# First modulation by column quarters in a two-block transformer kernel: VectorE alone from the second quarter on, masks and root moved

## The chip, the cores and the metric

One core of a Trainium2 chip runs the whole program: two transformer blocks on one sequence of 256 tokens, model width 2048, all in float32. The metric is device time in microseconds (us) of one execution; lower is better.

## The reference, cut to what matters

```
mod = silu(c) @ w_ada + b_ada             # 2048 x 12288, six sections
shift1, scale1, gate1, shift2, scale2, gate2 = split(mod, 6)
h = rms_norm(x, norm1_w) * (1 + scale1) + shift1
aq, ak, av, gq, gf, gi, gg = split(h @ w_in)          # seven parts of 1024 columns
attn = rms_norm(dilated_attention(rope(norm(aq)), rope(norm(ak)), av))
hg   = rms_norm(hgrn2(gq, gf, gi)) * silu(gg)         # gated linear recurrence
x = x + gate1 * (concat(attn, hg) @ w_out)
x = x + gate2 * (relu(mod2(rms_norm(x)) @ w_ff1)**2 @ w_ff2)
# then a second block: stick-breaking attention and another MLP
```

Only the first lines matter here: the projection input h needs `shift1` and `scale1`, which are 4096 columns of a product of a 2048-vector with 33.5 MB of `w_ada`.

## The kernel before, in words

Every large matrix product runs on TensorE in single-pass fp32r with a split of both sides: A = A_hi + A_lo and w = w_hi + w_lo, three matmuls for each tile (L257 to L259). A **chunk** is 512 rows by 512 columns of weights (1 MB): SyncE loads it to `raw` (`load`, L448), ScalarE rounds it to `w_hi` (`split_hi`, L243), VectorE takes the rest to `w_lo` (`split_lo`, L247), and TensorE does 24 matmuls with it. There are four slots, so load, w_hi and w_lo of a chunk wait for users of the chunk four before. Chunks are counted through the kernel. Chunks 0 to 11 are the first attention group (`at0_chunk`): three column blocks (q, k, v; b = 0, 1, 2) by four row blocks k, each of which needs a quarter of A. 12 to 23 are the second attention group, 24 to 55 the two groups of the recurrence. A **slot** s is the step of each engine's loop at which TensorE works on chunk s; the attention of a group (`at_stage`) is spread over the slots of the group behind it, and its norms (`at_own`) over its own last ones (`at_steps`): ScalarE squares, VectorE sums heads, GpSimd takes the power -0.5 (`power`), ScalarE scales by it, VectorE rotates, TensorE turns.

**The start.** `w_ada` for shift1 and scale1 comes by pieces through the SyncE queue: a piece is 128 rows with 1024 columns of each of the two sections (h = 0, 1: the column halves; k = 0 to 15: the rows), 1 MB, in a ring of four slots `ada_raw`. VectorE multiplies a piece by its entries of silu(c) and adds it to `MS` (L1087, L1089). Pieces named in `ADA_BY_PE` (three in the first half, two in the second) are multiplied by TensorE with one-column matmuls instead (`piece_sums`, L1669). SyncE issues a piece when its slot is free, in order; some chunks' loads stand between (`LOADS_AFTER`), some w_lo stand between VectorE's products (`LOW_AFTER`). When a half is summed, TensorE sums it over partitions and turns it into columns (`step_sums`, L1679), VectorE adds the bias (`step_modulation`, L1070, L1074). Eight steps give A, two row blocks of 128 each: TensorE transposes normalised X (L306), ScalarE scales and shifts from PSUM (L344) and rounds to A_hi (L347), VectorE gives A_lo (L364). Chunks 0 to 5 use the first half of A, 6 to 11 the second, in the order of `AT0_ORDER`.

VectorE also does, ahead of the first piece, the attention's counts and masks (L949 to L970), and between pieces the five level masks of the recurrence (L1005), X's row squares and root (L1018) and the bounds and angles (L1029).

From slot 7 on, the other w_ada columns (gate1, shift2, scale2) come in 0.5 MB pieces through X's memory, two for each slot (`ada_pieces`); VectorE adds them (L1141, L1144: 128x1024).

## Time and profile before

| | |
|---|---|
| median of 3 runs | 2432.97 us (2432.86 to 2433.14) |
| the profiled execution | 2433.19 us |
| its span in the trace | 2431.4 us |
| mean granted TensorE clock | 0.988 |

The profile is one execution. Times in its rows are from the start of the span; "idle before" and an arrow name what ended an engine's wait. Where a row groups instructions, the second number is the time from the first one's start to the last one's end.

### The profile page before, as it was taken

Reading aid. Unit: us, or ns where it says so; the run is one execution under the profiler, and the core shown is the slowest. Engines: PE = TensorE matmul, PEld = TensorE weight load, DVE = VectorE, ACT = ScalarE, POOL = GpSimd, SP = SyncE. Lnnn points to the kernel's source line nnn. Section 1 sums busy time; section 2 is a strip of 40 time slices with the busy share of each in tenths; the row PEclk is TensorE's granted clock in tenths of the full one; section 3 lists DMA queues with packets and bytes.
Section 4 is the critical chain, followed back from the end, with each engine's and each line's share of the span. In section 5 each row is a group of like instructions: output and inputs, shape, how many; then the busy total and the mean of one; then the engine's idle time right before and its main releaser. Section 6 shows DMA issues by size and latency. Waiting matters only on the chain.

```text
span 2431.4 us, 27934 instructions
## 1 busy us (share of the span) xinstructions
PE 2359.0 (97%) x10954; PEld 1968.0 (81%) x10954; DVE 1594.6 (66%) x1284; ACT 1039.6 (43%) x890; POOL 51.4 (2%) x56
## 2 busy tenths in 40 slices
PE   4899999999999999999999999999999999999999
PEld 3777888887888888888887888878888888888887
DVE  7868989987666666655568456556555565565554
ACT  2245553435333333333334556664443433433432
POOL 1011000001000000000000000000000000000000
PEclk9789999999999999999999999999999999999999
DMA  9988987755676776655554545444555655555552
GB/s 355 362 300 311 361 311 268 252 199 169 231 241 231 234 242 224 224 190 181 183 190 171 177 160 168 156 138 158 183 191 183 191 184 192 189 188 190 190 189 104
DMA packets 235129, 520.30 MB, mean 214 GB/s; under 512 B 9705, under 2 KB 10162, under 8 KB 232370
## 3 DMA queue, kind: packets, MB, share of 16 engines
q1 hardware_dynamic: 234352, 519.15, 63.2%
q8 instruction: 49, 0.80, 0.1%
q10 hardware_dynamic: 706, 0.17, 0.0%
q14 instruction: 22, 0.18, 0.0%
HBM read 517.19 MB, written 2.10 MB: 214 GB/s over the span
## 4 chain that ended last, share of the span: by engine, by line
PE 90%; DVE 4%; DMA 2%; ACT 2%; issue 1%; DVEq 1%; POOL 1%; ACTq 0%; SPq 0%
PE PS L257 28%; PE PS L259 28%; PE PS L258 28%; DMA ada_raw<-in_w_ada_dram 2%; PE PS L1695 2%; PE PS L1734 1%; PE PS L1669 1%; DVE w_lo L247 1%; PE PS L306 1%; ACT w_hi L243 1%; POOL rstd L609 1%; PE PS L1679 1%; DVE ada_acc L1144 0%; DVEq L1511 0%; PE PS L1799 0%
## 5 line engine op out<-in xcount | busy, mean ns | idle before, releaser
L247 DVE TENSOR_TENSOR w_lo<-raw,w_hi 128x2048 fp32r<-128x2048 f32 x392 | 897.6, 2291 | 688.4 <-ACT w_hi L243 683.4
L243 ACT ACTIVATE w_hi<-raw 128x2048 fp32r<-128x2048 f32 x392 | 750.9, 1916 | 1149.1 <-PE PS L259 1137.7
L257 PE MATMUL PS<-w_hi,A_hi 128*128 128x512 f32 x2112 | 839.7, 398 | 10.0 <-DVE A_lo L361 3.5
L259 PE MATMUL PS<-w_hi,A_lo 128*128 128x512 f32 x2112 | 827.5, 392 | 0.0
L258 PE MATMUL PS<-w_lo,A_hi 128*128 128x512 f32 x2112 | 827.2, 392 | 0.0
L257 PEld LDWEIGHTS PS<-w_hi,A_hi 128*128 128x128 f32 x2112 | 400.6, 190 | 92.2 <-ACT qT L738 2.8
L259 PEld LDWEIGHTS PS<-w_hi,A_lo 128*128 128x128 f32 x2112 | 399.5, 189 | 84.9
L258 PEld LDWEIGHTS PS<-w_lo,A_hi 128*128 128x128 f32 x2112 | 400.4, 190 | 81.2 <-issue 1.0
L257 PE MATMUL PS<-w_hi,H_hi 128*128 128x512 f32 x1024 | 401.6, 392 | 2.0 <-issue 1.3
L259 PE MATMUL PS<-w_hi,H_lo 128*128 128x512 f32 x1024 | 398.9, 390 | 0.0
L258 PE MATMUL PS<-w_lo,H_hi 128*128 128x512 f32 x1024 | 398.5, 389 | 0.0
L257 PEld LDWEIGHTS PS<-w_hi,H_hi 128*128 128x128 f32 x1024 | 192.3, 188 | 41.9 <-issue 2.2
L259 PEld LDWEIGHTS PS<-w_hi,H_lo 128*128 128x128 f32 x1024 | 192.2, 188 | 40.3
L258 PEld LDWEIGHTS PS<-w_lo,H_hi 128*128 128x128 f32 x1024 | 192.4, 188 | 38.9
L1144 DVE SCALAR_TENSOR_TENSOR ada_acc<-X,sc,ada_acc 128x1024 f32<-128x1024 f32 x90 | 115.3, 1281 | 4.5
L609 POOL TENSOR_TENSOR rstd<-ssq,mhalf 128x8 f32<-128x8 f32 x20 | 44.7, 2234 | 1666.3 <-DVE ssq L419 1399.8
L1506 DVE TENSOR_TENSOR ACC<-ACC,PS 128x1024 f32<-128x1024 f32 x60 | 72.8, 1214 | 0.0
L1506 DVE TENSOR_TENSOR X<-X,PS 128x1024 f32<-128x1024 f32 x60 | 72.8, 1213 | 0.0
L1089 DVE SCALAR_TENSOR_TENSOR MS<-ada_raw,sc,MS 128x2048 f32<-128x2048 f32 x25 | 58.8, 2350 | 14.8 <-DMA ada_raw<-in_w_ada_dram 14.1
L1669 PE MATMUL PS<-sc,ada_raw 128*128 128x1 f32 x160 | 29.9, 321 | 29.4 <-DMA ada_raw<-in_w_ada_dram 29.4
L1669 PEld LDWEIGHTS PS<-sc,ada_raw 128*128 128x128 f32 x160 | 29.8, 290 | 30.0 <-DMA ada_raw<-in_w_ada_dram 15.7
L1477 DVE SCALAR_TENSOR_TENSOR ada_acc<-gate_w,sc,ada_acc 128x2048 f32<-128x2048 f32 x16 | 37.6, 2352 | 4.0 <-issue 4.0
(267 smaller groups left out, 1108.0 us busy)
## 6 DMA issues: line engine op xcount, KB each, us to landing
raw<-in_w_ff_dram SPq DMA_DIRECT2D x128, 1024.0 KB, 5.3
raw<-in_mlp_w_in_dram SPq DMA_DIRECT2D x64, 1024.0 KB, 5.4
raw<-in_mlp_w_out_dram SPq DMA_DIRECT2D x64, 1024.0 KB, 5.0
raw<-in_w_in_dram SPq DMA_DIRECT2D x56, 1024.0 KB, 8.1
X<-in_w_ada_dram SPq DMA_DIRECT2D x96, 512.0 KB, 5.7
raw<-in_sb_w_qkv_dram SPq DMA_DIRECT2D x48, 1024.0 KB, 5.1
ada_raw<-in_w_ada_dram SPq DMA_DIRECT2D x32, 1024.0 KB, 9.8
raw<-in_w_out_dram SPq DMA_DIRECT2D x16, 1024.0 KB, 6.6
```

The lines of the kernel that those rows point to most:

```text
L243: act.activation(w_hi[:, j, :, :], raw[:, j, :, :], ACT.Copy).then_inc(hi_rdy, 1)
L247: dve.tensor_tensor(w_lo[:, j, :, :], raw[:, j, :, :], w_hi[:, j, :, :].bitcast(F32), ALU.subtract).then_inc(lo_rdy, 1)
L257: pe.matmul(bank(pair + t), h, w_hi[:, j, k, :], start=first, stop=False)
L258: pe.matmul(bank(pair + t), h, w_lo[:, j, k, :], start=False, stop=False)
L259: mm = pe.matmul(bank(pair + t), l, w_hi[:, j, k, :], start=False, stop=last)
L609: pool.tensor_tensor(rstd[:, :], ssq[:, :], mhalf[:, :], ALU.pow).then_inc(rstd_rdy, 1)
L1089: ins = dve.scalar_tensor_tensor(out=MS[:, 1 - h, :], in0=sl, scalar=sc[:, k:k + 1], in1=MS[:, 1 - h, :], op0=ALU.mult, op1=ALU.add)
L1144: ins = dve.scalar_tensor_tensor(out=acc, in0=ada_ring[:, q % CH, :], scalar=sc[:, k:k + 1], in1=acc, op0=ALU.mult, op1=ALU.add)
L1477: dve.scalar_tensor_tensor(out=acc, in0=gate_w[:, half, :], scalar=c, in1=acc, op0=ALU.mult, op1=ALU.add).then_inc(gate_w_used, 1)
L1506: dve.tensor_tensor(ac, ac, PS[:, b:b + 2, :], ALU.add).then_inc(acc_read, 1)
L1669: mm = pe.matmul(bank(6, at, at + 1), ada_raw[:, k % CH, P * c:P * c + P], sc[:, k:k + 1], start=True, stop=True)
L1695: mm = pe.transpose(bank(first_bank + i, P * q, P * q + P), src[:, t, HD * h:HD * (h + 1)], ident[:, :])
```

## The change

- The first modulation goes by four column quarters of 512. A piece has 512 columns of each section, 0.5 MB; the ring has eight slots in the same memory. VectorE multiplies all but three pieces of the first quarter, which are TensorE's.
- For each quarter TensorE transposes the first of its two steps, sums the quarter (`quarter_sums`), in quarters 2 and 3 runs one chunk (2 and 5: the third that needs the quarter before), then transposes the second step once the modulation is there, and runs chunks 0 and 1; 3 and 4; 6, 7 and 8; none. Chunks 9 to 11 come behind the fourth quarter. `AT0_ORDER` is row block by row block. The chunk of column block 0 waits for A_lo in two parts.
- X's squares go to ScalarE; the root's arithmetic stands behind product (0,8). The level masks are drawn by GpSimd behind the first power. Counts and masks go to VectorE's slots 10 and 11. Bounds and angles stand at (2,5).
- Group 0's norm steps lie one to two slots later, both its turned tiles go through banks 6 and 7, its attention one slot later (`STAGE_LAG`); chunk 12 waits for the first scaling (`n_mul`).
- The 0.5 MB pieces of the other columns start at slot 10 instead of 7; slots 13, 21, 36, 37, 49 and 50 take three.

The core of the diff:

```diff
-AT0_ORDER = [(b, k) for h in range(2) for b in range(3) for k in (2 * h, 2 * h + 1)]
-HEAD = CH * 3 // 2
-ADA_BY_PE = (3, 7, 11), (7, 11)
-PRE_COLS = 0, 96
-SUM_AT = (0, 0), (6, 80), (6, 160), (7, 0)
-
-
-def ada_share(h, k, mine):
-
-    return sum((b in ADA_BY_PE[a]) == mine for a in range(2) for b in range(KT) if (a, b) <= (h, k))
-
-
-LOADS_AFTER = {(0, 9): 0, (0, 11): 1, (0, 13): 2, (1, 0): 3, (1, 2): 4, (1, 4): 5, (1, 6): 6, (1, 9): 7}
-LOW_AFTER = {(0, 12): 0, (0, 14): 1, (1, 2): 2, (1, 4): 3, (1, 6): 4, (1, 9): 5, (1, 10): 6, (1, 13): 7}
-
-
-HG1_SLOT = CH * (OUT0 - 4)
-LEVEL_SLOTS = (range(HG1_SLOT, HG1_SLOT + 7),) + 2 * (range(CH * OUT0 - 1, CH * OUT0 + 2),) + (range(CH * OUT0 + 3, CH * OUT0 + 4),)
+QUARTERS = D // NC_
+RING = 2 * CH
+AT0_ORDER = [(b, k) for k in range(QUARTERS) for b in range(3)]
+HEAD = 3 * (QUARTERS - 1)
+ADA_BY_PE = (3, 7, 11), (), (), ()
+STAGE_LAG = 1
+def ada_share(q, k, mine):
+    return sum((b in ADA_BY_PE[a]) == mine for a in range(QUARTERS) for b in range(KT) if (a, b) <= (q, k))
+LOADS_AFTER = {(0, 9): 0, (1, 0): 1, (1, 6): 2, (1, 10): 3, (2, 0): 4, (2, 5): 5, (2, 10): 6, (3, 0): 7, (3, 5): 8, (3, 10): 9}
+LOW_AFTER = {(0, 12): 0, (1, 4): 1, (1, 9): 2, (1, 14): 3, (2, 4): 4, (2, 9): 5, (2, 14): 6, (3, 4): 7, (3, 9): 8, (3, 14): 9}
+ADA_FROM = HEAD + 1
+ADA_NONE = range(CH * OUT0 - 1, CH * OUT0 + 2)
+ADA_ONE = tuple(range(CH * (OUT0 - 4), CH * (OUT0 - 4) + 7)) + (CH * OUT0 + 3,)
+ADA_THREE = 13, 21, 36, 37, 49, 50
...
+    def per(x):
+        return 0 if x < ADA_FROM or x in ADA_NONE else 1 if x in ADA_ONE else 3 if x in ADA_THREE else 2
+    first, last = sum(per(x) for x in range(slot)), 2 * ADA_SLOTS
+    return range(min(first, last), min(first + per(slot), last))
...
+QUARTER_BANKS = 6, 7
...
+        ada_slots = ada_raw[:, :, :].rearrange("p j (h n) -> p (j h) n", n=2 * NC_)
+        ada_sum_of = [setup[:, D + 2 * NC_ * i:D + 2 * NC_ * (i + 1)] for i in range(2)]
...
             b, k = AT0_ORDER[n]
-            if b == 0:
-                pe.wait_ge(a_lo, 2 * (k + 1))
-            chunk(pe, n // CH, n % CH, pairs[b], lambda i, t: A_hi[:, CH * k + i, P * t:P * t + P],
-                  lambda i, t: A_lo[:, CH * k + i, P * t:P * t + P], k == 0, k == CH - 1)
+            if b:
+                chunk(pe, n // CH, n % CH, pairs[b], lambda i, t: A_hi[:, CH * k + i, P * t:P * t + P],
+                      lambda i, t: A_lo[:, CH * k + i, P * t:P * t + P], k == 0, k == CH - 1)
+                return
+            j = n % CH
+            pe.wait_ge(lo_rdy, n + 1)
+            for i in range(CH):
+                if i % 2 == 0:
+                    pe.wait_ge(a_lo, 2 * k + i // 2 + 1)
+                for t in range(T):
+                    h, l = (x[:, CH * k + i, P * t:P * t + P] for x in (A_hi, A_lo))
+                    first, last = k == 0 and i == 0, k == CH - 1 and i == CH - 1
+                    pe.matmul(bank(pairs[b] + t), h, w_hi[:, j, i, :], start=first, stop=False)
+                    pe.matmul(bank(pairs[b] + t), h, w_lo[:, j, i, :], start=False, stop=False)
+                    mm = pe.matmul(bank(pairs[b] + t), l, w_hi[:, j, i, :], start=False, stop=last)
+            mm.then_inc(chunk_done, 1)
...
-                    sp.wait_ge(y_rdy, 4)
+                    sp.wait_ge(sum_rdy, 1)
...
+            for piece in range(QUARTERS * KT):
+                q, k = divmod(piece, KT)
+                if piece >= RING:
+                    q0, k0 = divmod(piece - RING, KT)
+                    if k0 in ADA_BY_PE[q0]:
+                        sp.wait_ge(ada_pe, ada_share(q0, k0, True))
+                    else:
+                        sp.wait_ge(ada_used, ada_share(q0, k0, False))
+                sp.dma_start(ada_slots[:, piece % RING, :].rearrange("p (s n) -> p s n", s=2),
+                             ada[:, k, 0:2, NC_ * q:NC_ * (q + 1)]).then_inc(ada_in[piece % RING], 16)
+                if (q, k) == (0, CH - 1):
+                    sp.dma_start(X[:, :, :], a["x"].rearrange("a (t p) d -> p (a t) d", p=P)).then_inc(x_in, 16)
+                if (q, k) in LOADS_AFTER:
+                    load_at0(LOADS_AFTER[q, k])
...
+            power(0)
+            for i, w in enumerate(LEVELS):
+                drawn = setup[:, 1024 + P * (i % 2):1024 + P * (i % 2 + 1)]
+                upper = drawn.rearrange("p (b two w) -> p b two w", two=2, w=w)[:, :, 1, :]
...
+                pool.tensor_copy(lv_mask[:, i, :], drawn).then_inc(level_drawn, 1)
+            for i in range(1, MIX_JOBS + 2):
...
+            act.wait_ge(x_in, 16)
+            act.wait_ge(ssq_set, 1)
+            for t in range(T):
+                act.activation(Y0[:, t, :], X[:, t, :], ACT.Square, accum_out=ssq[:, t:t + 1]).then_inc(row_sq, 1)
             act.wait_ge(rstd_rdy, POWER_OF[0])
             for c in range(4):
                 normalise(act, X, X, c)
-            for n in (0, 1):
-                split_hi(act, 0, n)
-            turn_act(act, 0, g1, mod[:, SHIFT1, :], turned, steps=ALL[:4], banks=FIRST)
-            for n in range(2, CH * 2):
-                split_hi(act, n // CH, n % CH)
-            turn_act(act, 0, g1, mod[:, SHIFT1, :], turned, steps=ALL[4:], first=4, banks=SECOND_STEPS,
-                     between={1: lambda: split_hi(act, 2, 0)})
-            split_hi(act, 2, 1)
+            split_hi(act, 0, 0)
+            for q in range(QUARTERS):
+                turn_act(act, 0, g1, mod[:, SHIFT1, :], turned, steps=(2 * q, 2 * q + 1), first=2 * q, banks=QUARTER_BANKS)
+                for n in range(3 * q + 1, 3 * q + 4):
+                    split_hi(act, n // CH, n % CH)
...
+            def counts():
+                dve.wait_ge(level_drawn, 5 * len(LEVELS))
...
+            def masks():
...
+                dve.wait_ge(row_sq, T)
...
+            def quarter_modulation(q):
+                n = len(ADA_BY_PE[q]) + 1
+                r0, kts = RA["norm1"][0] + 4 * q, slice(4 * q, 4 * q + 4)
+                sums = ada_part[:, q, 0:8]
+                dve.wait_ge(ada_pe, ada_share(q, KT - 1, True))
+                dve.wait_ge(ada_sum, q + 1)
+                dve.tensor_reduce(sums, bank(QUARTER_BANKS[1], 0, 8 * n).rearrange("p (c m) -> p c m", m=n), AX_X, ALU.add)
+                d()
+                dve.tensor_tensor(mod[:, SHIFT1:GATE1, kts], sums.rearrange("p (s k) -> p s k", s=2),
+                                  colA[:, 0:2 * KT].rearrange("p (s k) -> p s k", s=2)[:, :, kts],
                                   ALU.add).then_inc(mod_rdy, 1)
                 d()
                 dve.scalar_tensor_tensor(out=g1[:, kts], in0=mod[:, SCALE1, kts], scalar=1.0, in1=colA[:, r0:r0 + 4],
                                          op0=ALU.add, op1=ALU.mult).then_inc(g_rdy, 1)
+            def turn_first(step):
+                turn_dve(dve, 0, g1, mod[:, SHIFT1, :], turned, steps=(step,), first=step,
+                         banks=QUARTER_BANKS[step % 2:step % 2 + 1], tmp_at=step % 2)
...
+            for q in range(QUARTERS):
                 for k in range(KT):
+                    if k in ADA_BY_PE[q]:
                         continue
+                    piece = KT * q + k
+                    sl, acc = ada_slots[:, piece % RING, :], ada_sum_of[q % 2]
+                    dve.wait_ge(ada_in[piece % RING], 16 * (piece // RING + 1))
                     if k == 0:
+                        ins = dve.tensor_scalar(acc, sl, sc[:, k:k + 1], None, ALU.mult)
                     else:
+                        ins = dve.scalar_tensor_tensor(out=acc, in0=sl, scalar=sc[:, k:k + 1], in1=acc, op0=ALU.mult, op1=ALU.add)
                     ins.then_inc(ada_used, 1)
+                    if (q, k) == (0, 8):
                         first_root()
+                    if q and k == 0:
+                        quarter_modulation(q - 1)
+                    if q and k in (1, 2):
+                        turn_first(2 * (q - 1) + k - 1)
+                    if (q, k) == (2, 5):
                         dve.wait_ge(rstd_rdy, 1)
                         bounds_and_angles()
+                    if (q, k) in LOW_AFTER:
+                        n = LOW_AFTER[q, k]
                         split_lo(dve, n // CH, n % CH)
+                    dve.wait_ge(ada_used, ada_share(q, k, False))
...
+            for step in (KT // 2 - 2, KT // 2 - 1):
+                turn_first(step)
+            for n in range(len(LOW_AFTER), CH * 3):
+                split_lo(dve, n // CH, n % CH)
...
-                            at_stage(pi, s, False, None)
+                            at_stage(pi, s - STAGE_LAG * (i == 1), False, None)
+                    if i == 0 and s == HEAD + 1:
+                        counts()
+                    if i == 0 and s == HEAD + 2:
+                        masks()
+                    if i == 1:
+                        at_own(0, PROJ0, CH * 3 + s, True)
...
+            def quarter_sums(q):
+                n = len(ADA_BY_PE[q]) + 1
+                pe.wait_ge(ada_used, ada_share(q, KT - 1, False))
+                for c in range(8):
+                    at = n * c + n - 1
+                    mm = pe.matmul(bank(QUARTER_BANKS[1], at, at + 1), ada_sum_of[q % 2][:, P * c:P * c + P], ones[:, 0:1],
+                                   start=True, stop=True)
                 mm.then_inc(ada_sum, 1)
...
+            for q in range(QUARTERS):
+                for k in ADA_BY_PE[q]:
+                    piece_sums(q, k)
+                pe.wait_ge(y_rdy, q + 1)
+                turn(0, X, steps=(2 * q,), first=2 * q, banks=QUARTER_BANKS[:1])
+                quarter_sums(q)
+                if q in (1, 2):
+                    at0_chunk(pe, 3 * q - 1)
+                pe.wait_ge(mod_rdy, q + 1)
+                turn(0, X, steps=(2 * q + 1,), first=2 * q + 1, banks=QUARTER_BANKS[1:])
+                for n in ((0, 1), (3, 4), (6, 7, 8), ())[q]:
+                    at0_chunk(pe, n)
...
+                        if i == 1 and s == 0:
+                            pe.wait_ge(n_mul, 1)
+                            used[p] += 1
+                        elif s % CH == 0:
...
-        return {"square": (8, 10), "norm": (9, 11), "turn": (10, 12), "copy": (11, 12)}
+        return {"square": (10, 11), "norm": (11, 12), "turn": (12, 13), "copy": (13, 13)}
...
+    return (6, 6) if isinstance(n, int) and n == 0 else (0, 2)
```

## Rows read from the trace of the kernel before

**Rows 1.** The page: busy times, and the costliest groups of instructions.
```profile
PE 2359.0 (97%) x10954; PEld 1968.0 (81%) x10954; DVE 1594.6 (66%) x1284; ACT 1039.6 (43%) x890; POOL 51.4 (2%) x56
...
L247 DVE TENSOR_TENSOR w_lo<-raw,w_hi 128x2048 fp32r<-128x2048 f32 x392 | 897.6, 2291 | 688.4 <-ACT w_hi L243 683.4
L243 ACT ACTIVATE w_hi<-raw 128x2048 fp32r<-128x2048 f32 x392 | 750.9, 1916 | 1149.1 <-PE PS L259 1137.7
...
L1144 DVE SCALAR_TENSOR_TENSOR ada_acc<-X,sc,ada_acc 128x1024 f32<-128x1024 f32 x90 | 115.3, 1281 | 4.5
```
**Rows 2.** Busy time by windows: length, PE, PEld, DVE, ACT, POOL, PEclk, DMA share, GB/s.
```profile
85.00:110.00 25.00, 25.00 (x114) 21.10 (x113) 24.80 (x12) 6.56 (x4) 0.00 (x0) 0.86 1.01 392
110.00:120.00 10.00, 10.00 (x55) 9.03 (x55) 9.36 (x5) 1.11 (x1) 0.00 (x0) 0.83 0.45 181
...
125.00:131.00 6.00, 4.55 (x32) 3.88 (x30) 2.11 (x3) 1.04 (x3) 0.00 (x0) 0.94 1.05 409
```
**Rows 3.** VectorE in order of time: start, us, instruction, idle before.
```profile
4.00 0.36 DVE L952 TENSOR_SCALAR MS<-MS 128x384 int32<-128x384 int32 x1 [3.05 <-POOL MS L604]
...
10.65 0.28 DVE L974 COPY colA<-PS 128x128 f32<-128x128 f32 x1
...
19.89 0.28 DVE L1007 TENSOR_TENSOR MS<-MS 128x128 int32<-128x128 int32 x1
...
24.45 2.29 DVE L1022 CUSTOM_DVE_ANT_0 raw<-X 128x2048 f32<-128x2048 f32 x1
...
29.15 7.13 DVE L1089 SCALAR_TENSOR_TENSOR MS<-ada_raw,sc,MS 128x2048 f32<-128x2048 f32 x3
...
43.62 0.16 DVE L1032 TENSOR_TENSOR turned<-turned 128x8 f32<-128x8 f32 x1
...
45.73 0.06 DVE L1049 MEMSET w_cols<- 32x2 f32 x1
...
72.91 0.17 DVE L1070 TENSOR_TENSOR mod<-PS,ada_part 128x8 f32<-128x8 f32 x1 [2.34 <-PE PS L1679]
...
76.84 1.29 DVE L364 TENSOR_TENSOR A_lo<-turned,A_hi 128x512 fp32r<-128x512 f32 x2
...
124.43 2.35 DVE L1089 SCALAR_TENSOR_TENSOR MS<-ada_raw,sc,MS 128x2048 f32<-128x2048 f32 x1 [3.96 <-DMA ada_raw<-in_w_ada_dram]
...
163.56 2.66 DVE L1144 SCALAR_TENSOR_TENSOR ada_acc<-X,sc,ada_acc 128x1024 f32<-128x1024 f32 x2
```
**Rows 4.** TensorE in order of time.
```profile
69.30 6.99 PE L1679 MATMUL PS<-ones,MS 128*128 128x1 f32 x32 [10.28 <-DVE MS L1089]
...
136.70 0.78 PE L257 MATMUL PS<-w_hi,A_hi 128*128 128x512 f32 x1
...
174.70 0.79 PE L257 MATMUL PS<-w_hi,A_hi 128*128 128x512 f32 x1 [2.41 <-ACT qT L738]
...
222.52 0.90 PE L1786 MATMUL PS<-ident,E 128*128 128x128 f32 x3 [2.85 <-ACT E L780]
```
**Rows 5.** The chain that ended last, in order of time: start, us, what.
```profile
177.63 0.43 PE PS L257
...
179.28 0.23 PE PS L257
```
**Rows 6.** ScalarE in order of time.
```profile
33.05 5.01 ACT L317 ACTIVATE X<-X,rstd 128x512 f32<-128x512 f32 x8 [18.53 <-POOL rstd L609]
...
73.44 1.02 ACT L344 ACTIVATE turned<-PS,mod,g 128x256 f32<-128x256 f32 x2 [20.13 <-DVE g L1074]
74.53 0.63 ACT L347 ACTIVATE A_hi<-turned 128x512 fp32r<-128x512 f32 x1
...
157.77 2.17 ACT L713 ACTIVATE QN<-PS,rstd 128x128 f32<-128x128 f32 x8 [0.69 <-POOL rstd L609]
```
**Rows 7.** GpSimd in order of time.
```profile
29.29 3.72 POOL L609 TENSOR_TENSOR rstd<-ssq,mhalf 128x8 f32<-128x8 f32 x1 [25.32 <-DVE ssq L1025]
```
**Rows 8.** A window around slots 49 and 50, columns as in rows 2.
```profile
425.00:450.00 25.00, 25.00 (x139) 21.53 (x138) 23.21 (x22) 11.24 (x12) 1.64 (x1) 1.00 0.77 267
```

More of the change, by code:

```diff
@@ L350, in turn_act, with turn_dve @@
                     between[pos]()
-        def turn_dve(dve, n, g, s=None, tmp=None, steps=ALL, first=0, banks=WIDE, between=None):
+        def turn_dve(dve, n, g, s=None, tmp=None, steps=ALL, first=0, banks=WIDE, between=None, tmp_at=0):
             dve.drain()
@@ L1075, in step_modulation @@
                                          op0=ALU.add, op1=ALU.mult).then_inc(g_rdy, 1)
-            def turn_first(steps, first, **more):
-                turn_dve(dve, 0, g1, mod[:, SHIFT1, :], turned, steps=steps, first=first, **more)
-            for h in range(2):
+            def turn_first(step):
+                turn_dve(dve, 0, g1, mod[:, SHIFT1, :], turned, steps=(step,), first=step,
+                         banks=QUARTER_BANKS[step % 2:step % 2 + 1], tmp_at=step % 2)
+            for q in range(QUARTERS):
```

201 lines of the change are left out of this document (57 added, 144 removed).

## The prediction

> **What bounds the kernel now.** Read the page first: TensorE is busy for 2359.0 us, 97% of the span [rows 1]. So only where TensorE idles, runs at its low clock or does work that could go away can time be won, and nearly all of that lies before the last modulation of projection input A. The edit is wholly in that start and in the first groups behind it.
>
> Next the windows [rows 2]. From 85 to 110 us VectorE is busy 24.8 of 25 us while DMA moves 392 GB/s: both are near their limits. From 110 to 120 DMA falls to 181 GB/s. The in-order SyncE queue explains it: piece (1,15) may go out only when TensorE's product of piece (1,11) has freed the slot, and that product stands behind the fifth chunk. The last product therefore starts at 124.43 and ends at 126.78, after 3.96 us of waiting for its load [rows 3]. Then come sums, A's second half, and six chunks from 136.70 to 172.29, where the next stall (2.41 us) begins [rows 4].
>
> Small prices. A matmul follows the last one after 0.43 us at 1.2 GHz and after 0.23 us at 2.4 GHz [rows 5]. A chunk of 24 is 5.46 us at the high clock. Six are 32.8; the 35.6 us from 136.70 to 172.29 leave 2.8, the turning of QN and some 9 slow matmuls at 0.2 more each: about 2 us, to be paid whenever TensorE has idled for over 2 us. After its 2.41 and 2.85 us of idleness the next matmul was slow again [rows 4].
>
> **What the change saves.** When the last product ends, three chunks are left instead of six: 3 x 5.46 = 16.4 us off the path. Between last product and first chunk lay 136.70 - 126.78 = 9.9 us (two sets of sums, four steps). Now: sums of one quarter 3.5 us (16 records; 32 took 6.99 [rows 4]), reduce, modulation and scale 0.65 (from the add at 72.91 to ScalarE's start at 73.44 it was 0.53, and a reduce of 0.2 more is my estimate), shift and copy on ScalarE 1.02 + 0.63 and gaps 0.2, A_lo half of 1.29 [rows 3, 6]: 6.7 us, since chunk 9 starts with its first step. That saves 3.2 us more. The change wins if the last product ends less than 19.6 us after 126.78.
>
> **When the last product ends.** It is a chain on VectorE.
>
> Its load: 61 products of 128x1024. That form took 1281 ns [rows 1], and two in a row 2.66 [rows 3], so 1.28 to 1.38 from start to start; I take 1.33, as this same loop left gaps of 0.04 at 2048 columns (three in 7.13 [rows 3]). The bounds give -3 and +3 us over 57 of them. Before, 27 products of 2.39 were 64 us; now 57 of 1.33 and four first ones of about 0.8 are 79. Two halves cost 0.27 us more than the one they replace, and TensorE's five pieces shrink to three halves. Ten w_lo instead of eight stand before the end, at 2.29 us [rows 1], 2.2 from start to start. Removed in front: masks 4.00 to 10.65, level masks 19.89 to 24.45, squares to 29.1, some 15.8 us [rows 3]. But these lay where the loads set the pace, so they buy little.
>
> First quarter. X now has 2.1 MB less before it: at about 0.41 MB/us that is 5.1 us before 24.45, so 19.4. ScalarE squares twice, bounded by one w_hi pass each (1.92 [rows 1]; with an accumulator 2.1): 23.5. The root stands behind product (0,8), whose load lies five pieces (6.3 us) behind X: 27.3. Pow 3.72 [rows 7], four normalisations 5.01 [rows 6], w_hi(0) 1.92: 38.0. w_lo(0) stands in VectorE's queue behind (0,12), whose load lies four pieces and one of w_in (7.6 us) behind (0,8)'s and which is done at 34.7; VectorE waits 3.3 us, and products 13 to 15 wait behind it. w_lo 2.3 and three products 4.0: the quarter ends at 44.3. Were w_hi(0) there in time, it would be 41.
>
> Each later quarter, from the end e of the last. The first product (0.8) hides in the sums, at e+3.65; modulation to e+4.2; product 1 to e+5.5; A_hi at e+6.05, A_lo to e+6.7; product 2 to e+8.05; second A_lo to e+8.7. Thirteen products 17.3 and three w_lo 6.6: 32.6 us.
>
> In quarters 3 and 4 there is something else: chunks 2 and 5 stand on TensorE between the sums and the second step's turning. VectorE waits for that step's A_hi right after product 2. TensorE has idled some 12 us (its chunks of the quarter before are done 17 us into a quarter of 32), so the chunk costs 7.3 us: e+3.55+7.3, transposes 0.5, ScalarE 1.8, gives A_hi at e+13.1 where VectorE wants it at e+8.05. That is 5.1 us twice, with all products and splits behind it. If the chunk ran at the high clock throughout, 3.2 twice.
>
> Quarter 3 has the bounds and angles too, 2.2 us (43.62 to 45.79 [rows 3]). So: 44.3 + 32.6 + (32.6+5.1+2.2) + (32.6+5.1) = 154.5 us. Does DMA hold it up? A quarter needs 8.4 MB of pieces and three chunks of w_in, 11.5 MB: 28 us at 0.41. Its packets shrink from 4 to 2 KB, but the window 125 to 131, when only 2 KB rows of w_in were moved, shows 409 GB/s [rows 2]. No: VectorE's 32.6 is longer. SyncE's added waits (loads 4 to 9 of w_in wait for w_lo four chunks back, in front of later pieces) pass at once by the order of splits: each w_lo wanted lies over eight pieces earlier, the ring's depth.
>
> **Up to chunk 12.** First chunk at 161.2, three chunks with 2 us of low clock: 179.6. Chunk 12 now waits for the first ScalarE scaling of QN (banks are turned elsewhere). VectorE does A_lo to e+8.7, w_lo of 10, 11, 12 (the first waits 0.9 for ScalarE) to e+16.3, then the counts (seven of the fourteen mask instructions, about 3.7 of the 6.65 us) with the head sum of 1.5 behind them: e+21.5. Pow 3.7 and norm 2.17 [rows 6, 7]: 181.9. So 2.3 us stall, as 2.41 before [rows 4]; chunk 12 starts at 182.0 instead of 174.70: 7.3 us late. Counts and masks are taken from 4 us, where nothing hung on them, and lie here, where VectorE has no slack.
>
> **Behind it.** Slots 12 to 23 of the first group's attention. VectorE starts them later than before against TensorE: 3 us of masks, and two slots of three pieces (2.7 us). Before, one wait of TensorE for a softmax row of 2.85 us stood there [rows 4]. I expect one more of the kind, with slow matmuls 4.5, and 0.7 at KN's bank: 5.2. Bounds: 0, if slack takes it all, and 10 for two more. The other four extra pieces (5.3 us) lie in slots 36, 37, 49, 50; VectorE was busy 23.2 of 25 us around the last two while TensorE never idled [rows 8]. I take them as hidden by what VectorE runs ahead: 0, and 5.3 if that cover is gone. Level masks on GpSimd run while VectorE waits: 0.
>
> One thing on that. Pow on GpSimd ran from 29.29 to 33.0 beside three VectorE products that kept 2.35 each [rows 3, 7]. The Trainium skill (SBUF — State Buffer, "Who interferes with whom") says that a VectorE instruction with two SBUF inputs and a GpSimd instruction that reads SBUF exclude each other for the whole instruction. By that rule the first quarter would lose up to the 3.7 us of pow, and the time would be 2449. This trace doesn't agree, so the sum stays with 0.
>
> **Sum.** 7.3 + 5.2 = 12.5 us later. The profiled execution took 2433.19 us (span 2431.4 and 1.8 around it), 0.22 above the median of 2432.97; 2432.97 + 12.5 = 2445.5.
>
> **Rivals.**
> (a) VectorE keeps pace with the loads: faster. By DMA alone the 46 MB up to piece (3,15) end at about 122, the last product at 124. Then 16.4 + 3.2 + 3 would be won, less 2 to 5 behind: 2413. For it: DMA and VectorE were both nearly full before [rows 2], and of the two only VectorE's share can be read wrongly by its waits. Against: 79 us of products, 23 of w_lo and the waits. It decides when the last product ends before about 140.
> (b) Same: w_hi(0) is early (-3), third chunks run fast (-4), and no further stall in the attention (-5): about 2434 to 2437.
> (c) Slower by more: VectorE stays the bound in slots 12 to 50, two further softmax stalls and the four pieces exposed: 12.5 + 5 + 5 = 22, 2455. For it: VectorE's 23.2 of 25 us [rows 8]. Against: TensorE's clock there was 1.00 throughout.
> (d) The change doesn't do what it says: chunks 6 to 8 don't fit before the last sums. Chunk 8 needs its w_lo after (3,9), done 10 us before the end; it fits. If one were left, +5.5: 2451.
>
> **Chances.** Forecast (2440 to 2450) 0.5; (b) 0.17; (c) and (d) 0.2; (a) 0.13. The range leaves out most of (a) and the far end of (c): 2431 to 2456. A difference under 0.2% (4.9 us) can't be told from none. Faster 0.12; same 0.14, most of (b); slower 0.74.
>
> **What the profile will show.** VectorE's first-quarter products end near 44, the others near 77, 117, 154. Rows of A_lo waiting 5 us on A_hi twice. TensorE: a chunk right behind sums at 80 and 120; idle about 12 us before both; chunk 9 near 161, chunk 12 near 182 with a stall of 2 us. Behind the second group all starts 12 to 13 us later than before, by a constant shift. I am wrong if the last product ends before 145, if a product of 1024 columns takes far from 1.33, or if the shift still grows after 270 us.

## The result and the profile after

The changed kernel takes 2448.26 us (median of 3 runs, 2448.22 to 2449.42) against 2432.97: ratio 1.0066, 95% interval [1.0049, 1.0083], slower by 15.3 us. The forecast was 12.5 us.

The page of the changed kernel, the lines that answer to [rows 1]. TensorE is 15 us less busy in a span 15 us longer, so its idle time grew by 30 us. Half of that is busy time that it no longer has: 112 matmuls fewer, those of its pieces (five of 32 matmuls before, 29.9 us; three of 16 now, 10.7 us). The products of 1024 columns take 1284 ns, and 17.6 us is all that VectorE waited in front of them.
```profile
PE 2344.1 (96%) x10842; PEld 1947.1 (80%) x10842; DVE 1601.2 (65%) x1302; ACT 1042.5 (43%) x894; POOL 63.0 (3%) x79
...
L252 DVE TENSOR_TENSOR w_lo<-raw,w_hi 128x2048 fp32r<-128x2048 f32 x392 | 897.5, 2291 | 682.3 <-ACT w_hi L248 677.1
...
L1103 DVE SCALAR_TENSOR_TENSOR MS<-ada_raw,sc,MS 128x1024 f32<-128x1024 f32 x57 | 73.2, 1284 | 17.6 <-DMA ada_raw<-in_w_ada_dram 14.7
```
Its windows, two of those of [rows 2] and the one of [rows 8]. From 85 to 110 us VectorE was busy 24.8 of 25 us before and now 19.4, and DMA moves 234 GB/s where it moved 392: both stand and wait for something else.
```profile
85.00:110.00 25.00, 15.40 (x70) 12.01 (x69) 19.43 (x32) 7.06 (x6) 0.00 (x0) 0.90 0.71 234
110.00:120.00 10.00, 3.10 (x15) 3.10 (x15) 7.53 (x6) 0.00 (x0) 0.00 (x0) 0.50 1.05 405
...
425.00:450.00 25.00, 25.00 (x137) 21.61 (x137) 23.15 (x20) 11.07 (x10) 0.00 (x0) 1.00 0.87 307
```
VectorE in order of time shows what it waits for. At 38.31 the first w_lo waits for ScalarE, with the quarter's last three products behind it. At 90.43 and 130.65 the second A_lo of quarters 3 and 4 waits for A_hi. The last products of quarters 2 to 4 start at 75.96, 115.57 and 153.96.
```profile
38.31 2.37 DVE L252 TENSOR_TENSOR w_lo<-raw,w_hi 128x2048 fp32r<-128x2048 f32 x1 [1.97 <-ACT w_hi L248]
...
75.96 1.28 DVE L1103 SCALAR_TENSOR_TENSOR MS<-ada_raw,sc,MS 128x1024 f32<-128x1024 f32 x1
...
90.43 0.69 DVE L381 TENSOR_TENSOR A_lo<-turned,A_hi 128x512 fp32r<-128x512 f32 x1 [4.80 <-ACT A_hi L364]
...
115.57 1.28 DVE L1103 SCALAR_TENSOR_TENSOR MS<-ada_raw,sc,MS 128x1024 f32<-128x1024 f32 x1
...
130.65 0.69 DVE L381 TENSOR_TENSOR A_lo<-turned,A_hi 128x512 fp32r<-128x512 f32 x1 [5.41 <-ACT A_hi L364]
...
153.96 1.28 DVE L1103 SCALAR_TENSOR_TENSOR MS<-ada_raw,sc,MS 128x1024 f32<-128x1024 f32 x1
...
174.47 1.22 DVE L1272 TENSOR_REDUCE ssq<-QN 128x8 f32<-128x1024 f32 x1
...
175.85 2.28 DVE L252 TENSOR_TENSOR w_lo<-raw,w_hi 128x2048 fp32r<-128x2048 f32 x1
```
TensorE in order of time, to be read with [rows 4]: two long idle times before sums, chunk 9 at 161.64, chunk 12 at 181.89 (174.70 before), then three more waits in the first group's attention.
```profile
77.29 3.57 PE L1696 MATMUL PS<-ones,MS 128*128 128x1 f32 x16 [11.48 <-DVE MS L1103]
...
116.91 3.58 PE L1696 MATMUL PS<-ones,MS 128*128 128x1 f32 x16 [14.58 <-DVE MS L1103]
...
161.64 0.77 PE L299 MATMUL PS<-w_hi,A_hi 128*128 128x512 f32 x1 [1.77 <-DVE A_lo L381]
...
181.89 0.50 PE L262 MATMUL PS<-w_hi,A_hi 128*128 128x512 f32 x1 [1.50 <-ACT QN L746]
...
195.84 1.06 PE L1713 MATMUL PS<-ident,KN 128*128 128x128 f32 x8 [1.81 <-ACT qT L771]
211.11 0.90 PE L1806 MATMUL PS<-ident,E 128*128 128x128 f32 x3 [2.62 <-ACT E L813]
240.96 0.55 PE L1806 MATMUL PS<-ident,E 128*128 128x128 f32 x3 [3.02 <-ACT E L813]
...
268.06 1.03 PE L1713 MATMUL PS<-ident,KN 128*128 128x128 f32 x8
287.13 0.55 PE L1806 MATMUL PS<-ident,E 128*128 128x128 f32 x3 [1.02 <-ACT E L813]
...
445.86 1.04 PE L1713 MATMUL PS<-ident,QN 128*128 128x128 f32 x8
```
The last two of these turnings in the kernel before are those of KN at 255 us and of a later QN. The shift is 7.2 us at chunk 12, 13.0 at KN, 15.4 at 446 us, and 15.1 over the span.
```profile
255.02 1.03 PE L1695 MATMUL PS<-ident,KN 128*128 128x128 f32 x8
...
430.47 1.04 PE L1695 MATMUL PS<-ident,QN 128*128 128x128 f32 x8
```

### The profile page after: what moved, and what is told of

Same layout as the page of the kernel before. It is cut to its first block, busy times and chain, and to the rows that moved or that the text cites. A ratio compares the mean times of both kernels' runs of the same rounds, so it can differ in the third digit from the quotient of the medians.

```text
span 2446.5 us, 27826 instructions
## 1 busy us (share of the span) xinstructions
PE 2344.1 (96%) x10842; PEld 1947.1 (80%) x10842; DVE 1601.2 (65%) x1302; ACT 1042.5 (43%) x894; POOL 63.0 (3%) x79
## 4 chain that ended last, share of the span: by engine, by line
PE 84%; DVE 8%; issue 3%; ACT 2%; DVEq 1%; DMA 1%; POOL 0%; ACTq 0%; SPq 0%
PE PS L262 26%; PE PS L264 26%; PE PS L263 26%; DVE MS L1103 2%; DVE w_lo L252 2%; PE PS L1713 2%; DVE ada_acc L1152 1%; PE PS L1752 1%; DMA ada_raw<-in_w_ada_dram 1%; ACT w_hi L248 1%; PE PS L1696 1%; PE PS L323 0%; POOL rstd L624 0%; DVEq L1527 0%; PE PS L1819 0%
## 5 line engine op out<-in xcount | busy, mean ns | idle before, releaser
L262 PE MATMUL PS<-w_hi,A_hi 128*128 128x512 f32 x2080 | 825.7, 397 | 14.5 <-DVE w_lo L252 7.2
L264 PE MATMUL PS<-w_hi,A_lo 128*128 128x512 f32 x2080 | 814.1, 391 | 0.0
L263 PE MATMUL PS<-w_lo,A_hi 128*128 128x512 f32 x2080 | 813.9, 391 | 0.0
L262 PEld LDWEIGHTS PS<-w_hi,A_hi 128*128 128x128 f32 x2080 | 393.4, 189 | 97.0 <-DVE w_lo L252 8.4
L264 PEld LDWEIGHTS PS<-w_hi,A_lo 128*128 128x128 f32 x2080 | 392.8, 189 | 83.5
L263 PEld LDWEIGHTS PS<-w_lo,A_hi 128*128 128x128 f32 x2080 | 393.3, 189 | 79.8 <-issue 1.0
L1103 DVE SCALAR_TENSOR_TENSOR MS<-ada_raw,sc,MS 128x1024 f32<-128x1024 f32 x57 | 73.2, 1284 | 17.6 <-DMA ada_raw<-in_w_ada_dram 14.7
L1696 PE MATMUL PS<-ones,MS 128*128 128x1 f32 x64 | 13.6, 342 | 34.5 <-DVE MS L1103 34.5
L361 ACT ACTIVATE turned<-PS,mod,g 128x256 f32<-128x256 f32 x16 | 8.1, 557 | 89.4 <-DVE g L1086 78.3
L1696 PEld LDWEIGHTS PS<-ones,MS 128*128 128x128 f32 x64 | 13.2, 315 | 35.7 <-DVE MS L1103 35.7
```

What stands on the lines that cost most here:

```text
L262: pe.matmul(bank(pair + t), h, w_hi[:, j, k, :], start=first, stop=False)
L263: pe.matmul(bank(pair + t), h, w_lo[:, j, k, :], start=False, stop=False)
L264: mm = pe.matmul(bank(pair + t), l, w_hi[:, j, k, :], start=False, stop=last)
L1103: ins = dve.scalar_tensor_tensor(out=acc, in0=sl, scalar=sc[:, k:k + 1], in1=acc, op0=ALU.mult, op1=ALU.add)
L1696: mm = pe.matmul(bank(QUARTER_BANKS[1], at, at + 1), ada_sum_of[q % 2][:, P * c:P * c + P], ones[:, 0:1], start=True, stop=True)
```

## The experiments

My theory was the prediction's: in the start VectorE is one chain; the third chunk of quarters 1 and 2 holds it up twice, masks and counts come at a bad place, and the 16 us of chunks taken off the path don't pay for that. The rivals are that DMA with its smaller packets sets the pace, or that TensorE does. Each ratio below is to the kernel before, run beside that version. With 3 or 4 runs of a version its interval reaches some 4 us to each side. So where two such versions lie 2 us apart, their times don't show the difference, and only the rows can tell where it comes from.

**The third chunk before the sums.**
```
-                if q in (1, 2):
-                    at0_chunk(pe, 3 * q - 1)
-                for n in ((0, 1), (3, 4), (6, 7, 8), ())[q]:
+                for n in ((0, 1, 2), (3, 4, 5), (6, 7, 8), ())[q]:
```


> Undoes one part of the change: chunks 2 and 5 of the first projection run before the next quarter's sums instead of between them and the second step's turning. My theory (VectorE is a chain in the start, and the third chunk holds back its A_lo twice): the waits of 4.80 us at 90.43 and 5.41 us at 130.65 vanish, VectorE's last product ends near 144 instead of 155.2, chunk 12 starts near 171 to 172, and the whole shift of about 10 us stays through the second group: about 2438 us. Rival 1 (VectorE's lateness is only in appearance; w_lo and the pieces of the loads set the pace, so something else ends last): the two waits vanish, but VectorE waits for loads in their place and the last product still ends after 150: 2444 or more. Rival 2 (the third chunk hid in time in which TensorE would idle anyway, so moving it before the sums makes TensorE late for the sums): the sums begin later than VectorE's last product of a quarter and nothing is won: about 2448.

Measured: 2438.28 us (2435.41 to 2441.06, 10 runs), ratio 1.0023 [1.0013, 1.0032]. The waits of 4.80 and 5.41 us are gone; the last sums start at 143.61, for which 144 was expected, and chunk 9 at 150.67. The theory holds and both rivals fall; the interval lies wholly below that of the changed kernel. But the lead isn't kept: at KN this kernel is only 0.5 us behind the kernel before, at 436.48 it is 6.0 us behind, after another softmax wait. Its TensorE rows:
```profile
143.61 3.58 PE L1696 MATMUL PS<-ones,MS 128*128 128x1 f32 x16 [3.66 <-DVE MS L1103]
150.67 0.77 PE L299 MATMUL PS<-w_hi,A_hi 128*128 128x512 f32 x1 [1.78 <-DVE A_lo L381]
...
255.50 1.04 PE L1713 MATMUL PS<-ident,KN 128*128 128x128 f32 x8
...
276.18 0.90 PE L1806 MATMUL PS<-ident,E 128*128 128x128 f32 x3 [2.63 <-ACT E L813]
...
436.48 1.04 PE L1713 MATMUL PS<-ident,QN 128*128 128x128 f32 x8
```

**Counts and masks in front.**
```
+            dve.wait_ge(pool_const, N_CONST)
+            counts()
+            masks()
...
-                    if i == 0 and s == HEAD + 1:
-                        counts()
-                    if i == 0 and s == HEAD + 2:
-                        masks()
```


> Undoes one part of the change: counts and masks are made by VectorE at about 4 us, as in the kernel before, instead of in the first group's slots. My theory: the quarters end as in the changed kernel (44.5, 77.2, 116.9, 155.2, each within 0.5), the head sum comes 3.6 us earlier, so the stall of 1.50 us before chunk 12 goes, and with the masks out of slot 14 the wait at the turning of KN of the second group is reached 3 to 5 us earlier: 2443.5 to 2445.5. Rival 1 (this work also hides beside something here): the stall goes, but the softmax waits of 2.62 and 3.02 us grow by as much: 2447 to 2449. Rival 2 (the front isn't free: VectorE's first products or the squares wait for it): the first quarter ends later by up to 6 us, and the time is 2448 to 2452.

Measured: 2445.92 us (1.0055 [1.0038, 1.0072]), 2.3 us less than the changed kernel, which the intervals don't separate. In the rows the stall before chunk 12 is gone and KN of the second group turns at 264.59 (3.5 us earlier), but the second softmax wait grew from 3.02 to 4.45 us. The places are the theory's; its range (2443.5 to 2445.5) is missed by 0.4 us, and some of rival 1 is in it.

**TensorE multiplies two pieces of each quarter.**
```
-ADA_BY_PE = (3, 7, 11), (), (), ()
+ADA_BY_PE = (3, 7, 11), (7, 11), (7, 11), (7, 11)
```


> Undoes one part of the change: TensorE multiplies pieces 7 and 11 of quarters 2, 3 and 4 too, so VectorE has 6 products of about 1.3 us fewer. Theory A (VectorE's own work sets the start's length from product to product): the last product ends 7 to 8 us earlier and the time is about 2440 to 2441. Theory B (the same chain, but a slot that TensorE reads comes free only when TensorE comes to it, and pieces 7 and 11 are read before the quarter's first step, so the fewer products only bring VectorE sooner to waits for loads or for A_hi, which still hang on the sums and the third chunk): quarter ends 2 to 5 us earlier, time 2443 to 2446. Rival (TensorE's reading of the pieces stands in front of its turning, waits for loads and delays the second step by more than it saves): no gain or a loss, 2448 to 2455.

Measured: 2446.48 us (1.0058 [1.0041, 1.0075]). This is theory B, a little outside its ranges (2 to 5 us, 2443 to 2446): sums of quarters 2, 3 and 4 start 2.8, 5.4 and 4.8 us earlier (74.52, 111.50, 150.47), and VectorE now waits 3.85 us for a load before its last product. Six products less gave 1.8 us in the end, which the intervals don't separate from none.

**All three.**
The edits of the three experiments above together.

> Undoes three parts at once: the third chunk before the next sums, masks and counts in front, TensorE multiplying two pieces of each quarter. What remains is the split into four quarters with the squares on ScalarE, the level masks on GpSimd and the later turning. My theory, the shifts being separate and added as far as the loads let them: the last product ends near 140, chunk 12 starts near 164 to 166, the shift against the changed kernel is 16 to 18 us: 2430 to 2433, level with the kernel before or a little under. Rival 1 (with VectorE relieved, DMA sets the end of the start): the last product still ends after 145 with VectorE waiting for loads for 5 us and more in quarters 3 and 4: 2436 to 2442. Rival 2 (four quarters win outright once VectorE is relieved, 16 us of chunks being off the path): under 2425.

Measured: 2443.57 us (1.0046 [1.0029, 1.0063]). My sum of 2430 to 2433 failed: this version is 5 us slower than the one with the third chunk alone. Rival 1 named the place (loads late in quarters 3 and 4), but its range of 2436 to 2442 is missed too. VectorE waits for loads in quarters 2 to 4:
```profile
77.41 1.28 DVE L1105 SCALAR_TENSOR_TENSOR MS<-ada_raw,sc,MS 128x1024 f32<-128x1024 f32 x1 [3.88 <-DMA ada_raw<-in_w_ada_dram]
...
115.27 1.28 DVE L1105 SCALAR_TENSOR_TENSOR MS<-ada_raw,sc,MS 128x1024 f32<-128x1024 f32 x1 [5.50 <-DMA ada_raw<-in_w_ada_dram]
...
150.39 1.28 DVE L1105 SCALAR_TENSOR_TENSOR MS<-ada_raw,sc,MS 128x1024 f32<-128x1024 f32 x1 [2.25 <-DMA ada_raw<-in_w_ada_dram]
```
By its name this is a shortage of DMA. The waits of SyncE's queue from 20 to 170 us say otherwise: 40.8 us in which the next load waited for TensorE's reading of an old piece.
```profile
SPq L484 <- PE PS L1684: 40.8, 5, 13.5
```

**Third chunk and masks, VectorE alone.** The edits of the first two experiments together.

> Undoes two parts of the change (third chunk before the next sums, counts and masks in front at 4 us), and keeps the third: VectorE alone multiplies from the second quarter on. Together with the version that undid all three (2443.6 us, last product late because VectorE waited for loads 3.88, 5.50 and 2.25 us) it isolates TensorE's pieces. Theory A (a slot that TensorE is to read stands behind a chunk in TensorE's queue, and so holds back the loads behind it; with VectorE alone the slots come free in time): the loads are there, last product near 144 as with the third chunk alone, and the two gains add: 2435 to 2437 us. Rival B (masks in front cost more here, because they make the squares and the first loads late once nothing else is): 2438 to 2440. Rival C (what held the version with all three was DMA itself and not the slots): VectorE waits for loads here as well, last product after 148, 2441 or more.

Measured: 2433.74 us (2430.48 to 2435.89, 11 runs), 1.0002 [0.9993, 1.0011], better than the sum of the two and than the 2435 to 2437 expected. The last sums start at 143.44 (151.73 with TensorE's pieces), no product after 40 us waits a microsecond for its load, and the same row of SyncE's queue is:
```profile
SPq L484 <- PE PS L1684: 3.1, 2, 1.6
```
So theory A holds. TensorE's pieces gave 1.8 us in the kernel that had the third chunk late, and cost 10 us in this one, since a chunk then stands in TensorE's queue before the reading that frees the slot. VectorE alone from the second quarter on is the part of the change that is worth having here.

This version also prices the masks a second time: against the one with the third chunk alone they are the only difference, 2438.28 to 2433.74 us, and these intervals lie apart. The third softmax wait fell from 2.63 us (at 276.18) to 1.03 (at 272.16), the shift at KN by 2.4 us and at the later QN by 5.6.

**Two slots of three pieces later.**
```
-ADA_THREE = 13, 21, 36, 37, 49, 50
+ADA_THREE = 30, 33, 36, 37, 49, 50
```


> As the one before (third chunk before the sums, masks in front), and the two slots of three pieces that lie at 13 and 21, between the first softmax rows, are moved to 30 and 33. The number of pieces is the same. Theory A (from chunk 12 to 25 VectorE has no slack: a w_lo of 2.2 and two products of 2.67 per chunk of 5.46, and each row of softmax that it makes late stops TensorE for some 2.6 us and brings back the low clock): at least one of the three softmax waits seen in the version with the third chunk alone (200.16, 230.01, 276.18) goes or all shrink, 2 to 4 us less than the version before: 2432 to 2434. Rival B (these waits are the chain transposition, softmax on ScalarE and back, whatever VectorE does): the same waits, the same time within 1 us. Rival C (the pieces hurt as much at 30 and 33): the wait at 276 grows, time the same or up to 2 us more.

Measured: 2433.88 us (1.0003 [0.9994, 1.0012]), no difference from the version before. The two softmax waits were 1.22 and 4.63 instead of 2.61 and 3.14, a third of 1.03 vanished, and at KN the profiled execution was 3.1 us ahead (249.96 to 253.08), of which 1.2 were there at chunk 9 already. Then this stood at 371 us:
```profile
371.43 2.05 PE L1750 MATMUL PS<-bT,kT 128*128 128x128 f32 x16 [2.65 <-DVE kT L1209]
```
The time lies in theory A's range (2432 to 2434), but only because the version before was faster than that range took for granted: the 2 to 4 us between them aren't there, and the lead at KN is given back at the wait at 371 us.

**The same move in the changed kernel.** (The same one-line edit.)

> The changed kernel with one move: the slots of three pieces at 13 and 21 lie at 30 and 33. Tests my term of 5.2 us for waits in the first group's attention (measured 2.62 at 211.11, 3.02 at 240.96, 1.02 at 287.13). Theory A (two products of 1.33 us in slots without slack cause part of these waits): second group's KN turned 2 to 3 us earlier than 268.06. Rival B (VectorE's whole amount of work up to slot 48 is what counts, so the lead is given back): KN at 268 earlier by 2 to 3 but a wait of 2 to 3 us appears at 370 to 390 and the time is within 1 us of 2448.3. If theory A alone: 2445 to 2446.5. If neither: KN at 268.

Measured: 2449.94 us (1.0076 [1.0061, 1.0092]); KN at 267.70, only 0.4 earlier, waits of 1.21 and 4.63 where there were 2.62 and 3.02, and 2.65 at 389.20. It is not faster; rival B's return of the lead is seen, on a lead that was hardly there. The slots of three pieces decide which of the two softmax waits is the long one, and not their sum (5.84 us here, 5.64 in the changed kernel).

**w_lo of chunk 0 behind product (0,15).**
```
-LOW_AFTER = {(0, 12): 0, (1, 4): 1, (1, 9): 2, (1, 14): 3,
+LOW_AFTER = {(0, 15): 0, (1, 4): 1, (1, 9): 2, (1, 14): 3,
```


> The changed kernel with one move: w_lo of chunk 0 behind product (0,15) instead of (0,12). Tests my term for the first quarter: VectorE stood 1.97 us at w_lo(0) for ScalarE's w_hi(0), with three products and the quarter's sums behind it. Theory A (that wait and the split itself lie on the path of the first quarter): sums of quarter 1 start near 40.5 to 41.5 instead of 44.58, later quarters 3 to 4 us earlier throughout, about 2444.5 to 2446. Rival B (the loads of pieces 13 to 15 set that end): VectorE waits for loads instead, the sums start at 43 or later, within 1.5 us of 2448.3. Rival C (the gain is swallowed before the second quarter ends, since the loads of quarter 2 aren't there yet): quarter 1 ends early, quarter 2 ends at 76 or later.

Measured: 2446.32 us (1.0050 [1.0035, 1.0066]). Sums of quarter 1 start at 40.69 instead of 44.58, which is theory A at that place (its range of times, 2444.5 to 2446, is missed by 0.3 us). Of the 3.9 us, 3.1 are left at the last sums but one and 2.7 at the last, because the waits behind the third chunk grow (5.54 and 5.86), and 1.9 in the time, which the intervals don't separate from none.

**The kernel before, piece (1,11) read one chunk earlier.**
```
-                if n in (2, 4):
-                    piece_sums(1, ADA_BY_PE[1][n // 2 - 1])
+                if n in (2, 3):
+                    piece_sums(1, ADA_BY_PE[1][n - 2])
```


> The kernel before with one move: TensorE reads piece (1,11) behind its fourth chunk instead of its fifth. Tests the reading of the load that came late there (VectorE's last product waited 3.96 us for piece (1,15), which may go out only when piece (1,11) has been read). Theory A (the slot behind TensorE's chunk held the load back): the slot is free 5.5 us earlier, the wait of 3.96 us goes, the last product starts near 120.5 instead of 124.43, and as TensorE's sixth chunk then ends last (near 124.6), the sums start some 2 us earlier: 2430 to 2431 against 2432.4. Rival B (DMA was the limit and the slot of no matter): product (1,15) starts at 123 or later, time unchanged within 0.5 us. Rival C (piece (1,11) isn't there yet at 109 and TensorE waits for it): the sixth chunk ends later, 2433 to 2436.

Measured: 2431.65 us (11 runs), 0.9991 [0.9982, 1.0001], which can't be told from none. The mechanism shows: the last product has no wait any more and starts 2.56 us earlier (124.43 in [rows 3]), though all rows of this execution lie 1.1 us later from 70 us on. The wait of 3.96 us was the slot's, not DMA's. The sums that follow gained little (they start at 127.76 against 127.05, in an execution that lies 1.1 us later), because TensorE's sixth chunk ends just before them in both.
```profile
121.87 2.35 DVE L1089 SCALAR_TENSOR_TENSOR MS<-ada_raw,sc,MS 128x2048 f32<-128x2048 f32 x1
...
130.08 0.17 DVE L1070 TENSOR_TENSOR mod<-PS,ada_part 128x8 f32<-128x8 f32 x1 [5.86 <-PE PS L1679]
```

**What helped, together.** With the two slots moved:

> All that has helped so far: third chunk before the next sums, masks in front, the two slots of three pieces at 30 and 33, and w_lo of chunk 0 behind product (0,15). In the changed kernel the last move alone brought sums of quarter 1 from 44.58 to 40.69 us and 2 us in the end. Theory A (VectorE's stream sets the pace from the start to slot 48, so that what it gains in the first quarter stays): everything from the second quarter to 450 us lies 2.5 to 4 us earlier than in the version without the move (QN turned at 429.45 there), time 2430 to 2432, under the kernel before by 1 to 3 us. Rival B (loads of the second quarter or a row of softmax eat it): second quarter's sums at 77, or another wait near 371 us that grows: 2433 to 2435.

and with them in their place:

> Third chunk before the sums, masks in front, w_lo of chunk 0 behind (0,15), and the slots of three pieces where the changed kernel has them (13, 21). Against the version just before it tells what moving the two slots is worth, against the version without the move of w_lo (2433.7 us) what that move is worth. Theory A: 2 to 3 us under the 2433.7, 2431 to 2432. Rival B (the move gives nothing once the third chunk lies earlier): 2433.5 to 2434.5. If the slots at 30 and 33 only delay the same deficit of VectorE (a wait of 2.65 us appeared at 371 us there), both versions come out within 0.5 us of each other.

Measured: 2431.80 us, 0.9993 [0.9984, 1.0002], and 2430.51 us (2427.63 to 2431.21, 11 runs), 0.9989 [0.9980, 0.9998]. The second (third chunk before the sums, masks in front, w_lo(0) late) is the fastest, 2.3 us under the kernel before beside it, and 17.8 under the changed one. It isn't clear of the version with the slots moved (1.3 us), nor of the kernel before with piece (1,11) read earlier (2431.65 us, a change of two lines). The move of w_lo is worth 3.2 us there, by intervals that just overlap. Its rows: 
```profile
40.91 3.57 PE L1694 MATMUL PS<-ones,MS 128*128 128x1 f32 x16 [2.14 <-DVE MS L1105]
...
145.66 0.77 PE L299 MATMUL PS<-w_hi,A_hi 128*128 128x512 f32 x1 [1.77 <-DVE A_lo L381]
...
249.35 1.04 PE L1711 MATMUL PS<-ident,KN 128*128 128x128 f32 x8
...
427.15 1.04 PE L1711 MATMUL PS<-ident,QN 128*128 128x128 f32 x8
```
It starts chunk 12 at 164.70, 10.0 us ahead of the kernel before (174.70), reaches KN 5.7 us ahead, is 3.3 ahead at 427 us and 2.3 in the time. So the start in four quarters wins 10 us, and the slots behind it give three quarters of that back.

**VectorE waits for GpSimd's root.**
```
                 if s == steps["square"][0]:
                     head_norm(n, 0, QN, 0, 1.0 / SCALE ** 2, rotate, not rotate, meanwhile)
+                    if isinstance(n, int) and n == 0:
+                        dve.wait_ge(rstd_rdy, 2)
```


> The changed kernel; VectorE, after the first head sum of QN, waits for GpSimd's root before it goes on with w_lo of chunk 12. Tests whether GpSimd is kept waiting by VectorE. The root before head scaling of QN took 3.61 us (176.03) beside w_lo (175.85, 2.28 us), and the root at 354.78, beside which VectorE did nothing, 1.64. Theory A (GpSimd's root stands until VectorE's instruction with two operands is through, and VectorE loses nothing by it): the root takes 1.64, ends 2 us earlier, and chunk 12 starts up to 1.5 us earlier, without its stall of 1.50 us; VectorE is 1.8 us later behind it, which softmax waits may take back: 2446 to 2449. Theory B (the root takes 3.6 us in this place whatever VectorE does, its input or code being cold): 3.6 us again, VectorE 3.7 us later, 2448 to 2452.

Measured: 2450.28 us (1.0071 [1.0054, 1.0087]). The root took 1.64 us, and chunk 12 starts at 181.12 with no stall of a microsecond or more: theory A, in the mechanism. Its time lies above theory A's 2446 to 2449: KN's turning then waited 4.66 us instead of 1.81, VectorE being 2 us later with everything behind, and the version isn't faster than the changed one. The root in this kernel (first line), and in the changed one:
```profile
176.81 1.64 POOL L624 TENSOR_TENSOR rstd<-ssq,mhalf 128x8 f32<-128x8 f32 x1 [130.36 <-DVE ssq L1275]
```
```profile
176.03 3.61 POOL L624 TENSOR_TENSOR rstd<-ssq,mhalf 128x8 f32<-128x8 f32 x1 [130.25 <-DVE ssq L1275]
...
354.78 1.64 POOL L624 TENSOR_TENSOR rstd<-ssq,mhalf 128x8 f32<-128x8 f32 x1 [104.68 <-DVE ssq L436]
```

## Why the prediction was right, step by step

- **The chain on VectorE.** Forecast ends of the last products 44.3, 76.9, 117 and 154.5; measured 44.5, 77.2, 116.9 and 155.2. The start to start time of 1.33 us was 1.32 (five in 6.56). In the first quarter two errors cancelled: X's root was computed at 28.50 instead of 27.3, but its power took 2.69 us (at 28.74) and not the 3.72 of [rows 7], so that w_hi(0) was there at 38.3 where 38.0 was forecast. That product (0,12) came at 35.05 instead of 33.3 cost nothing: it only made the wait for w_hi(0) 1.97 us instead of 3.3. "Were w_hi(0) there in time, it would be 41" was shown by the move of w_lo (40.69), though there w_lo itself left the path too.
- **The third chunk.** Forecast 5.1 us twice, measured 4.80 and 5.41; taking it away gave 11.7 us at the last sums (155.29 to 143.61) and 10.0 in the time. It is the largest of the parts of the loss that were undone one by one. The chunk itself took 7.3 us and 7.9 (7.3 was taken), the first eight and eleven of its matmuls at a granted clock of 0.50.
- **DMA.** "No: VectorE's 32.6 is longer" holds: without TensorE's pieces and without the third chunk a quarter took 32.3 us (111.35 to 143.61 between its sums) and from the second quarter on no product waited as much as 0.7 us for a load.
- **Up to chunk 12.** Forecast 7.3 us late with a stall of 2.3; measured 7.2 and 1.50. The masks are behind the stall: with them in front it is gone. In the time they are worth 2.3 us alone, inside the intervals, and 4.5 us with the third chunk early, outside them. Chunk 12 came with no low clock behind that stall (matmuls 0.23 us apart from 182.24 on), which the sum hadn't counted on.
- **Behind it.** Forecast 5.2, measured 13.0 - 7.2 = 5.8: the turning of KN 1.81 (0.7 was taken), softmax 2.62 and 3.02 against one of 2.85. These waits are 4.6 of the 5.8 us; no wait of 0.6 us or more holds the rest. The number was near, and two of its reasons weren't right: the slots of three pieces moved away changed KN by 0.4 us, and the extra slow matmuls (4.5 - 2.85 = 1.65 of the 5.2 us) didn't come: 13 matmuls of 512 columns took 0.6 us or more in this stretch, and 13 in the kernel before.
- **Slots 24 to 62** is the term that was mis-sized: 0 taken, 5.3 as its bound; measured 15.4 - 13.0 = 2.4, of which 1.86 stand in a softmax wait of 1.02 at 287.13 and a wait for VectorE of 0.84 at 387.83; the rest is in no wait of that size. With it the sum would have been 14.9. The prediction names this as a sign of being wrong ("if the shift still grows after 270 us"), and it did grow: in the reading of these slots the prediction was wrong, and it was right in the number because the term is small. Every version with four quarters gives way in the same stretch (against the kernel before, 1.7 to 5.9 us between the turnings at 255 and 430 us). VectorE is busy 21 to 24 of 25 us in the windows from 250 to 450 us, in the changed kernel and in the fastest version, and so it is in the kernel before, where no such wait stands; moving its pieces to and fro gives nothing. That VectorE comes into this stretch late and can't catch up there is argued from this and not shown; nearest to a test comes the return of the masks, which takes work away from it ahead of the stretch and cut the growth from 5.5 us to 2.4 with the third chunk early, but left it (2.4 and 2.6 us) where that chunk came late.
- **The rule weighed.** The Trainium skill (SBUF — State Buffer, "Who interferes with whom") was set aside because VectorE's products kept their length. They did here too (1284 ns). But the sign was on the other engine: it is the row of 3.72 us in [rows 7] itself. The root takes 1.64 us where VectorE stands still, 3.61 when it is issued behind a w_lo (176.03 against 175.85), and 1.64 again when VectorE was made to wait. The runs agree with the rule, and here GpSimd pays. As the sum had 3.7 us for the root before chunk 12, taken from that row, this misreading cost it nothing there. The 2449 that the prediction gave for it is near the measured time by chance: it laid the loss on VectorE's products in the first quarter, which kept their length. What lay on that quarter's path is the root's own stretch, 2.69 us against 1.64, as w_lo(0) waited for what follows the root.
- **Rivals.** (a) needed the last product before 140; it was 155.2, and the fastest version has it at 139.7 and wins 2.3 us, not 20, because the lead of 10.0 us that it has at chunk 12 doesn't outlive slots 12 to 62. (b) and (d) didn't happen. Of (c) a part did: more than one softmax wait, and a shift that grew behind slot 24, by 2.4 us and not 5.
- **Low clock.** The prediction pays 2 us of it "whenever TensorE has idled for over 2 us". The runs don't bear out that condition: chunk 12 of the kernel before ran at a granted clock of 0.50 behind 2.41 us of idleness, and of 1.00 behind 2.43 us in the version with the early read. In the changed kernel the wait of 2.31 us before 136.73 left the clock at 1.00.

It stays open how much of the lead's loss is VectorE's amount of work and how much the order of stages behind the first group, which now lie one slot later. No run changed that order, and none undid the squares on ScalarE or the level masks on GpSimd.

## What to carry over

When a wait is named for a load, look in the issuing queue for what the load waited on: 40.8 us of "DMA" were TensorE's queue. Costs of parts don't add: TensorE's two pieces of each quarter gave 1.8 us in one version and cost 10 in another, so undo parts in pairs before blaming one. A lead in the start has to be followed to the end: of 10.0 us at chunk 12, 2.3 were left. And work put between an engine's sums and its next step (a chunk of 7.3 to 7.9 us at the clock left by idling) costs every engine queued behind that step.
